# Transposing the normalized activations with the DMA crossbar instead of TensorE

## The reference

```python
h = rmsnorm(x, norm_g)
proj = h @ w_in + b_in                    # 1024 -> 2816 columns
q, k, v, z_a, u_s, v_s, z_s = split(proj) # 512,128,128,512,512,512,512
attn = banded_sink_attention(q, k, v, sinks) * silu(z_a)      # window 128, 8 heads, 2 kv heads
sgu = chunked_spatial_gating(gelu(u_s), gelu(v_s), ...) * silu(z_s)  # LayerNorm(v), 128x128 W_s per head
x = x + concat(attn, sgu) @ w_out + b_out
return rmsnorm(x, final_norm_g)
```

## Time and profile before

| | |
|---|---|
| median of 3 timed runs | 592.85 us (592.27 to 593.55) |
| profiled execution, its own time | 591.91 us |
| its span, slowest core | 590.3 us (8 cores: 586.1 to 590.3) |
| PE busy | 525.3 us, 89% of the span |
| DVE, ACT, POOL busy | 346.3 us (59%), 331.8 us (56%), 263.7 us (45%) |
| mean granted clock of TensorE | 0.970 on this core |

### The profile page before, as it was taken

One profiled execution on the slowest core, in us unless ns is written; L12 is line 12 of the kernel. 1 busy time (PEld: TensorE's weight loads), 2 busy tenths in 40 slices (PEclk: granted clock), 3 DMA queues, 4 the chain that ended last, 5 costly groups with the idle time before them and its releaser, 6 DMA issues.

```text
span 590.3 us, 9639 instructions; the slowest of 8 cores (586.1 to 590.3 us)
## 1 busy us (share of the span) xinstructions
PE 525.3 (89%) x3150; PEld 238.7 (40%) x3150; DVE 346.3 (59%) x428; ACT 331.8 (56%) x570; POOL 263.7 (45%) x289
## 2 busy tenths in 40 slices
PE   1799547999899989999899989999899989999962
PEld 1366312443453434443453434443453434543420
DVE  2765595464934486365934586265835577255754
ACT  4344635647664576637655576646755576337631
POOL 2013491350644536362553536362553536262482
PEclk9999876999999999999999999999999999999986
DMA  7999880300414024220415014230411023200352
GB/s 227 325 341 320 281 141 1 108 1 1 178 73 179 2 77 173 72 109 0 179 72 179 2 64 177 80 109 1 179 72 73 1 72 129 86 1 2 143 190 95
DMA packets 19059, 66.61 MB, mean 113 GB/s; under 512 B 2241, under 2 KB 2369, under 8 KB 19010
## 3 DMA queue, kind: packets, MB, share of 16 engines
q1 hardware_dynamic: 17714, 63.85, 30.7%
q0 software_dynamic: 1152, 2.10, 2.3%
q10 hardware_dynamic: 144, 0.05, 0.1%
HBM read 51.30 MB, written 16.78 MB: 115 GB/s over the span
## 4 chain that ended last, share of the span: by engine, by line
PE 60%; DVE 11%; ACT 10%; issue 9%; POOL 7%; DMA 2%; POOLq 0%; DVEq 0%; ACTq 0%; SPq 0%
PE pp L500 29%; PE pp L703 14%; ACT junk L455 4%; DVE vln L571 3%; PE pp L656 3%; PE pp L556 2%; PE pp L525 2%; PE pp L629 2%; PE pp L660 2%; DVE mixT L611 2%; POOL LR L675 2%; DMA xa<-x 2%; PE pp L599 2%; PE pp L539 1%; POOL st_lr L569 1%
## 5 line engine op out<-in xcount | busy, mean ns | idle before, releaser
L500 PE MATMUL pp<-xT,w_fm 128*128 128x512 bf16 x1088 | 246.5, 384 | 4.9 <-ACT vs_f L560 3.6
L500 PEld LDWEIGHTS pp<-xT,w_fm 128*128 128x128 bf16 x1088 | 104.3, 99 | 138.9 <-issue 21.7
L703 PE MATMUL pp<-w_out_bf,mixT 128*128 128x512 bf16 x512 | 123.3, 387 | 5.2 <-DVE mixT L679 5.2
L689 POOL TENSOR_TENSOR xe<-xe,bout_sb 128x1024 f32<-128x1024 f32 x32 | 81.8, 2558 | 6.4 <-DMA xe<-x 6.3
L703 PEld LDWEIGHTS pp<-w_out_bf,mixT 128*128 128x128 bf16 x512 | 46.7, 99 | 66.8 <-issue 21.7
L634 ACT ACTIVATE PT<-pp 128x1024 bf16<-128x1024 f32 x63 | 62.7, 1032 | 17.6 <-PE pp L629 17.6
L675 POOL TENSOR_TENSOR LR<-LR,zaT 128x512 f32<-128x512 f32 x32 | 38.1, 1190 | 77.2 <-ACT LR L673 77.2
L708 DVE TENSOR_TENSOR xe<-pp,xe 128x512 f32<-128x512 f32 x64 | 43.5, 685 | 43.7 <-PE pp L703 40.3
L717 DVE SCALAR_TENSOR_TENSOR xe<-xe,st_fr,gf_sb 128x1024 f32<-128x1024 f32 x32 | 46.3, 1446 | 27.2 <-POOL st_fr L715 26.7
L647 DVE TENSOR_TENSOR PT<-PT,pack_b_sb 128x1024 bf16<-128x1024 bf16 x56 | 55.4, 999 | 8.8 <-ACT PT L634 7.9
L669 ACT ACTIVATE LR<-pp,esink 128x128 f32<-128x128 f32 x128 | 36.5, 368 | 37.4 <-PE pp L660 37.4
(11 more groups left out here) (64 smaller groups left out, 609.1 us busy)
## 6 DMA issues: line engine op xcount, KB each, us to landing
xa<-x SPq DMA_DIRECT2D x32, 512.0 KB, 5.3
xe<-x SPq DMA_DIRECT2D x32, 512.0 KB, 3.5
out<-xe SPq DMA_DIRECT2D x32, 512.0 KB, 2.7
xe<-w_in SPq DMA_DIRECT2D x12, 512.0 KB, 12.0
mixT<-w_in SPq DMA_DIRECT2D x10, 512.0 KB, 14.2
w_out_bf<-w_out POOLq DMA_DIRECT2D x8, 256.0 KB, 9.2
LR<-sgu_wT SPq DMA_DIRECT2D x1, 512.0 KB, 17.5
bout_sb<-bout_bc SPq DMA_DIRECT2D x1, 512.0 KB, 18.4
```

The costliest lines, as they stand in the source:

```text
L500: ins = e.matmul(bank(h), lhsT=w_fm[:, FM.index(cb), k, :], rhs=xT[:, xb, k, :], start=(k == 0), stop=(k == 7))
L689: G.op("pool", lambda e: e.tensor_tensor(out=xe[:, s, :], in0=xe[:, s, :], in1=bout[:], op=ALU.add), reads=["c_bout"], writes=[("xe", s, 0 ...
L703: ins = e.matmul(bank(h), lhsT=mixT[:, mb, ec, tt * 128:(tt + 1) * 128], rhs=w_out[:, ec, hf * 512:(hf + 1) * 512], start=(ec == 0), stop= ...
```

## The change

For supertile 0 nothing changes. For supertiles 1 to 7 (28 tiles) `transpose_x` no longer makes eight TensorE transposes and a copy out of PSUM, but one DMA issued by SP, which reads the `xn` tile (128 x 1024 bf16, 256 KB) and writes the eight transposed 128x128 blocks to `xT`. Each `tt` has a semaphore of its own (`d_xt`). The planner gets an issue cost of 1.2 and a size of 512 KB for it.

```diff
+        d_xt = [sem(f"d_xt{i}") for i in range(4)]
...
         def transpose_x(st, tt):
-            h = Bank("P")
             xb = st % 2
+            if st:
+                G.op("sp", lambda e: e.dma_start_transpose(out=xT[:, xb, :, tt * 128:(tt + 1) * 128], in_=xn[:, tt % 3, :]),
+                     reads=[("xn", tt % 3)], writes=[("xT", xb, tt)], cost=1.2, dsem=d_xt[tt], kb=512, prio=st - 0.8 + 0.04 * tt)
+                return
+            h = Bank("P")
```

More of the change, by code:

```diff
@@ L477, in transpose_x @@
         def transpose_x(st, tt):
+            xb = st % 2
+            if st:
+                G.op("sp", lambda e: e.dma_start_transpose(out=xT[:, xb, :, tt * 128:(tt + 1) * 128], in_=xn[:, tt % 3, :]),
+                     reads=[("xn", tt % 3)], writes=[("xT", xb, tt)], cost=1.2, dsem=d_xt[tt], kb=512, prio=st - 0.8 + 0.04 * tt)
+                return
             h = Bank("P")
-            xb = st % 2
             def tr(e):
```

## The result

The changed kernel takes 574.56 us (median of 4 runs, 574.12 to 575.18) against 592.56 us (591.65 to 593.55) on the same chip: ratio 0.970, 95% interval 0.968 to 0.972, faster by 3%. The forecast was 580 us. The profiled execution took 574.95 us over a span of 573.1 us, 17.2 us less than the span before. Medians here are over all timed runs; in three kernels further down (changed with 4 `xn` buffers, fastest with supertile 1 on TensorE, each DMA three times) one run was 4 to 15% longer, with the cores of one die at a lower clock, and without it they take 571.53, 568.52 and 609.50 us; the ratios leave it out.

A forecast was written before the change was run, and what follows sets the result against it. It took TensorE to bound the steady supertiles. From the profiled 591.91 us, -11.4 - 10.1 + 4.8 + 4 = -12.7 gave 579.2, or 580 for the median of timed runs; own range 571 to 590, 8-in-10 range 570 to 640.

The forecast's parts named there:

- Transposes off TensorE: Steady supertiles: 32 transposes costing 1.90 us leave TensorE in each of six, -11.4 us.
- The wait of 1.68 us: TensorE's gap ahead of a values block, behind VectorE's scale of tile 3, goes in six supertiles: -10.1 us.
- The v_s chain: Gelu phase: W_s matmuls wait longer for the last `vln`, 0.8 us in each of six supertiles, +4.8 us.
- The first supertile: q, k, v matmuls of supertile 1 now stand behind supertile 0's attention: 0.9 gained to 10.6 added, +4 us taken.
- r: Time one transposing DMA holds the DMA engines or queue; 2.2 us taken, between 0.75 and 6.3.
- The sum 4r + 5.7: Queue time in us for a supertile's four transposes, three 512 KB loads and 1.2 us latency; 14.5 at r = 2.2.
- The cover itself: From tile 0 ready (about 186) to the first q group (205): 19 us hide the DMAs, up to r = 3.3.
- The second wait: VectorE's scale of tile 3 waits for the DMA of tile 0; binds only from r = 4.8 us.
- C: Rival: Gelu phase is set by the v_s chain, so TensorE's freed time turns into waits; 597 us, chance 0.11.
- B: Rival: transposes land late, r above 3.3 us, q waits in each of six supertiles; 601 us, chance 0.25.
- E: Rival: transposes land far later, r = 6.3 us, 11.9 us late per supertile; 651 us, chance 0.10.
- D: Rival: first supertile pays its full 10.6 us, the rest as forecast; 587 us, within the forecast's own 0.54.

The follow-up runs named there:

- fastest with supertile 1 on TensorE: Changed kernel with four `xn` buffers and three Gelu buffers from the third supertile on (566.21 us), but supertile 1 transposed by TensorE: 568.54 us.
- the pair with four buffers: The kernel before and the changed kernel, each with four `xn` buffers in place of three: 583.17 and 571.58 us.

## Why the forecast was right, and where it was off

The mechanism held; the sum was -12.7 us where the span shows -17.2. In the two traces the steady part is made up of 11.0 us less work of TensorE (383.8 to 372.8 us busy), 10.1 us less waiting at the values blocks and 3.7 us more at W_s and z_s together; the rest of the 17.55 lies in gaps too short for the table. By the steps of the forecast:

- **Transposes off TensorE, -11.4 us: right.** 11.0 by TensorE's busy time; the pair with four buffers gives 10.9 in the steady part.
- **The wait of 1.68 us, -10.1 us: right.** In the changed kernel all of it is gone. In the kernel before the scale alone, moved by the fourth buffer, is worth a little less, 6 x (66.51 - 65.12) = 8.3 us: 10.1 us of wait go, and 1.9 us of small waits at L656 and L703 come.
- **The v_s chain, +4.8 us: 3.7 net, near in size and incomplete in cause.** W_s waits 6.5 us more over six supertiles, z_s 2.8 us less, which the forecast had not counted. It had counted the lost cover, rightly: with 32 matmuls ahead again (each DMA twice) the wait is gone. The scale's 0.72 us count for little: moved away, the wait falls from 1.3 to 1.0 us. What it left out is the buffer of the fourth Gelu, which takes the wait down from 1.0 to 0.35 us. That release was in no term of the sum, though the trace before shows ScalarE waiting for it at the third and fourth Gelu:

```profile
187.93 0.60 ACT L560 ACTIVATE vs_f<-pp 128x512 f32<-128x512 f32 x1 [3.35 <-DVE st_mv L564]
191.79 0.60 ACT L560 ACTIVATE vs_f<-pp 128x512 f32<-128x512 f32 x1 [3.27 <-DVE vln L571]
```

- **The first supertile, +4 us: failed; 0.47 measured.** The step said that 10.6 us of matmuls are added if the same idle time stays. TensorE's work only changes its place there. What adds is new idle time, and that went from 87.45 - 69.26 = 18.2 us to 87.92 - 67.89 = 20.0 us, less 1.4 us of work. The wait of 6.00 us became 9.54, and the one of 11.53 fell apart into six of 0.4 to 2.9, 10.5 together. These 3.5 us are the larger part of the miss of 4.5.
- **r, 2.2 us taken between 0.75 and 6.3: 2.0 measured**, and (0.551 x 608.7 - 0.414 x 573.1) / 56 = 1.75 us for each additional one. **The sum 4r + 5.7 was a little too long:** from the first issue to the last landing it gives 13.7 us at r = 2.0 where 12.9 are measured (184.12 to 197.05), 20.8 at twice the work (r near 3.8) where 18.7 are, and 27.7 at three times (near 5.5) where 24.2 are. The cover itself, 19 us, is 20.1 in the changed kernel (184.12 to 204.21). So cover and work meet at r near 3.8, not 3.3, and three times the work is 4.46 us late. The second wait, of tile 3's scale for the DMA of tile 0, was to bind from r = 4.8; it shows at 3.8 in two supertiles, and once with single DMAs (supertile 1 on TensorE, 0.69 us).

**Rivals.** C falls by the pair with four buffers. B and E need r above 3.3 and near 6.3; the mean of a single transpose is 2.0, and three in place of one made B real, 18 us slower than before. D falls with the first supertile's term.

The two prices that the forecast took from the Trainium skill both differ from the 2.0 us measured for a tile. The effective rate of DMA: Bandwidth & Descriptors (Latency and other measured facts), which the page gives for a middle dimension that is not contiguous, made 1.0 us as an estimate; the traces do not agree. The crossbar's price of VectorE: DVE Perf Modes (The three transpose paths), taken eight times as an estimate, gave 10.5 us; they do not agree with that either, and the rule drawn from it, to use TensorE where PSUM will do, did not hold in this kernel, where TensorE is the bound and the DMA engines are not.

The forecast's signs are in the trace: steady supertiles of 63 to 65 us, no gap at the second values block, a first q group without wait. The landings after 3 to 4 us are there for most transposes (median 3.3 us), not for the fourth of a supertile, which takes 6.8 to 9.1 us in four of five. One of its warnings is in it too, the longer wait at W_s.

## What to carry to other kernels

Work moved from the engine that bounds a stretch to one that idles is worth nearly its whole time there (10.9 of 11.4 us here), as long as its result lands ahead of its reader; count that margin from the trace, for the last transfer and in the queue where it stands with its neighbours, not from the median. A buffer that the removed work freed late can be worth nearly as much as the work: try one more buffer by itself before the larger change, here 1.5% of the kernel's time came so. Where an engine waits anew, follow the chain back to the first instruction that waits for a buffer and not for data; there 5 us more were found.

## What the runs showed of the hardware

A wait can cost TensorE more than its length, and the length alone doesn't tell whether it does. In the kernel with three DMAs for one, the table by stretch has the granted clock behind the wait of 4.46 us (columns as above):

```profile
280.44:283.20 2.76, 2.75 (x15) 0.90 (x14) 0.22 (x1) 2.57 (x4) 0.00 (x0) 1.00 0.92 331
287.65:291.20 3.55, 3.55 (x10) 1.07 (x12) 0.00 (x0) 0.00 (x0) 0.00 (x0) 0.50 0.27 106
291.20:294.60 3.40, 3.40 (x15) 0.96 (x16) 2.04 (x3) 1.02 (x1) 0.00 (x0) 0.68 0.00 0
294.60:300.00 5.40, 5.40 (x31) 2.02 (x30) 2.81 (x3) 4.28 (x8) 1.15 (x1) 1.00 0.00 0
```

0.50 is the lower of the clock's two levels, 1.2 GHz; it takes until 294 us to be back at 2.4. Three groups of instructions behind the wait take 3.57 + 1.03 + 2.50 us and not 1.90 + 0.61 + 1.90, 2.7 us on top of 4.46. Behind the other three such waits (4.71, 4.40 and 4.60 us) the clock begins at 0.58, 0.51 and 0.50. Behind the waits of 1.50 us in the changed kernel the clock stays at 1.00. In the kernel with each DMA twice two waits of 1.92 us ahead of W_s end differently; the windows behind the first, then behind the second:

```profile
199.00:201.00 2.00, 2.00 (x6) 0.65 (x5) 1.20 (x2) 0.10 (x1) 1.63 (x2) 0.50 0.80 315
...
265.00:267.00 2.00, 2.00 (x11) 0.90 (x10) 1.24 (x2) 0.69 (x1) 1.68 (x2) 1.00 1.02 336
```

Behind the first, 32 matmuls take 8.77 us, behind the second 7.08; that makes the difference between its supertiles of 65.96 and 64.26 us. Behind the wait of 2.74 us in the kernel with supertile 1 on TensorE the clock stays at 1.00 too. What decides it no run here shows.

In the prologue, behind the loads of weights and x, SP stands in the issue of one transposing DMA for 11.9 us, and it lands 17.4 us after the issue began; in the steady part the longest issue is 1.9 us and the latest landing 9.1 us.
